# A decoder layer on one core: plain feed-forward tiles over all eight PSUM banks, and another order of VectorE's work before the block products

## The chip, the core and the metric

The kernel runs on one core of one Trainium2 chip. A core has TensorE (PE in the profile), VectorE (DVE), ScalarE (ACT), GpSimd (POOL) and SyncE (SP, which here only issues DMAs). They run side by side, each works through its own list in order, and semaphores tie the lists together. The metric is the device time of one launch in microseconds (us).

## What is computed

One decoder layer on x of 512 tokens by 1024 channels, all in float32: a half-step SwiGLU feed-forward part, a mixing part (pooling and windowed attention, gated and merged), and a second half-step feed-forward part. What the change touches is the feed-forward part, which runs twice:

```python
def swiglu(x, w_gate, w_up, w_down):
    return (jax.nn.silu(x @ w_gate) * (x @ w_up)) @ w_down
...
h = h + 0.5 * swiglu(rmsnorm(h, ffn1_norm), ffn1_w_gate, ffn1_w_up, ffn1_w_down)
...
h = h + 0.5 * swiglu(rmsnorm(h, ffn2_norm), ffn2_w_gate, ffn2_w_up, ffn2_w_down)
```

w_gate and w_up are 1024 x 2816, that is 22 tiles of 128 columns each.

## The kernel before

**Arithmetic.** Every float32 operand is split into a rounded "high" part and a "low" rest (operand minus high), both of type fp32r, and a product is three matmuls: high x high, high x low, low x high (lines 478 to 480 for 512 columns, 531 to 533 for 256). ScalarE makes the highs by copying, GpSimd or VectorE makes the lows by subtracting.

**The plain stage.** The first six tiles f = 0 to 5 of gate and up are multiplied directly. Each is two weight units, u = 2f for gate and 2f + 1 for up: eight slices of 128 x 128, 24 matmuls of 512 columns into one PSUM bank (`plain` and `project` in the tensor block). A unit's way is: SP loads it into one of four slots when the unit four before it has been used (`unit_used`), ScalarE makes its high (`next_unit`, line 850), GpSimd its low (`low_part`, line 1246), PE multiplies. The four banks 4 to 7 are used in turn: tile f writes banks 4 + 2k and 5 + 2k with k = f % 2, so that a unit of tile f waits for `gate_scaled` or `up_scaled` to reach f - 1. Those are counted by VectorE's `plain_scaled` (lines 1378 and 1382), which multiplies a bank by the norm factor rinv and so empties it. ScalarE then makes a tanh (`gate_tanh_tile`, line 878) and VectorE the hidden tile (`plain_hidden`, lines 1389 and 1393). The norm factor comes from a sum over the partitions that PE makes in bank 0 (`sum_of_squares`) and VectorE reads (`norm_factor`).

**The pairs.** The other 16 tiles are multiplied two by two, in eight pairs, by a scheme for 2 x 2 blocks with seven products in place of eight, seven for gate and seven for up. A block product is 12 matmuls of 256 columns, 14 products make a pair (numbered 0 to 13 in the order of `pair`): a11 and a12 of gate, a11 and a12 of up, s2 and s1 of gate, s2 and s1 of up, s3 and s4 of gate, s3 and s4 of up, a22 of gate, a22 of up. Their moving operands are blocks of the normalised input (B11, B21, B22) and four sums of them (NT2, NT1, T3, T4); VectorE builds them (`scale_blocks`, `sum_blocks`), ScalarE makes highs, and VectorE makes seven lows of 128 x 1024 (`block_low`, line 1419, `sum_low`, line 1424), which PE waits for by count (`moving`). Their weights are a1 (a11 and a12), s31 (s1 and s3), s2, s4 and a22. s31 is loaded by SP and then added to in place by an accumulating DMA from GpSimd's queue (`add_units`, line 1252); VectorE adds s2 and s4 from it (`weight_sums`, lines 1431 and 1433) and makes the lows of a1, s2 and s31 (`low_a1`, `low_s2`, `low_s31`, lines 1439, 1443 and 1447); GpSimd makes the "late" lows of s4 and a22 (lines 1257 and 1260). The up blocks of the first pair lie where the units 8 to 11 were, so that SP loads them only as these units are used (`up_prologue`).

**The parts of a pair.** PE adds later products onto banks 0 and 1, and ScalarE copies each intermediate state out (`copy_part`, line 909). PE's s2 of gate waits for the first copy. VectorE adds the copies up (`add_part`, line 1521): g0l and u0l, then g1r (which a22 of gate waits for), g0r, u1r (which a22 of up waits for) and u0r. Between u0l and g1r stand the weight sums and lows for the next pair.

The order on each engine is written out by hand. ScalarE's first part copy of pair 0 stands behind `gate_tanh_tile(5)` and the highs of up's s2 and s31, and waits for `hidden` to reach 6.

## Time and profile before

| | us |
|---|---|
| median of 3 runs | 1081.14 |
| lowest, highest | 1077.69, 1082.23 |
| the profiled execution | 1081.94 |
| its span, first to last instruction | 1080.1 |
| PE busy | 1051.6 |
| VectorE busy | 656.3 |
| ScalarE busy | 478.0 |
| GpSimd busy | 434.1 |
| PE's mean granted clock, of full | 0.992 |

All times in the text are counted from the start of the span. The first feed-forward part (FFN1) has its plain stage up to 89 us and its pairs behind that; the second (FFN2) has its plain stage at 725 to 792. A row of a timeline gives the start, the duration, the engine, the line in the kernel, the operation, what it writes and reads, and how often it follows itself. Rows of one engine overlap a little, since an instruction is let in before the one ahead has ended: the pace is the distance of starts. The idle time before an instruction, and what ended it, stand in brackets. Matmul starts are exact, their ends are modelled.

### The profile page before, as it was taken

Reading aid. Unit: us, or ns where it says so; the run is one execution under the profiler, and the core shown is the slowest. Engines: PE = TensorE matmul, PEld = TensorE weight load, DVE = VectorE, ACT = ScalarE, POOL = GpSimd, SP = SyncE. Lnnn points to the kernel's source line nnn. Section 1 sums busy time; section 2 is a strip of 40 time slices with the busy share of each in tenths; the row PEclk is TensorE's granted clock in tenths of the full one; section 3 lists DMA queues with packets and bytes.
Section 4 is the critical chain, followed back from the end, with each engine's and each line's share of the span. In section 5 each row is a group of like instructions: output and inputs, shape, how many; then the busy total and the mean of one; then the engine's idle time right before and its main releaser. Section 6 shows DMA issues by size and latency. Waiting matters only on the chain.

```text
span 1080.1 us, 15526 instructions
## 1 busy us (share of the span) xinstructions
PE 1051.6 (97%) x6024; PEld 914.7 (85%) x6024; DVE 656.3 (61%) x1008; ACT 478.0 (44%) x825; POOL 434.1 (40%) x240
## 2 busy tenths in 40 slices
PE   6889999999999999999999999999999999999998
PEld 5769999998888777887777788888889999998887
DVE  5899767758440276425676756668986667685101
ACT  6334555556331233335777653343344554553110
POOL 1433342335434435344454535444323423344441
PEclk9999999999999999999999999999999999999999
DMA  7434776733332422222111113216257757433232
GB/s 277 116 97 115 189 196 158 188 106 98 98 98 97 137 88 98 78 78 80 58 58 58 59 59 98 98 39 199 95 119 187 198 163 187 117 104 98 98 98 98
DMA packets 42033, 126.35 MB, mean 117 GB/s; under 512 B 4336, under 2 KB 4336, under 8 KB 41968
## 3 DMA queue, kind: packets, MB, share of 16 engines
q1 hardware_dynamic: 37216, 108.41, 30.3%
q0 software_dynamic: 4608, 16.78, 9.1%
q8 instruction: 45, 0.74, 0.3%
q10 hardware_dynamic: 144, 0.26, 0.1%
q14 instruction: 20, 0.16, 0.1%
HBM read 123.34 MB, written 2.10 MB: 116 GB/s over the span
## 4 chain that ended last, share of the span: by engine, by line
PE 80%; DVE 12%; ACT 3%; DMA 2%; issue 2%; SPq 0%; DVEq 0%; ACTq 0%
PE psum L478 16%; PE psum L480 15%; PE psum L479 15%; PE psum L531 10%; PE psum L532 9%; PE psum L533 9%; PE psum L755 1%; DVE gate L1389 1%; DVE moving_sums_low L1424 1%; PE psum L770 1%; DVE hidden L1393 1%; DMA w_raw<-weights_dram 1%; PE psum L783 1%; DVE u_blocks_low L1419 1%; PE psum L784 1%
## 5 line engine op out<-in xcount | busy, mean ns | idle before, releaser
L1246 POOL TENSOR_TENSOR w_low_in_place<-w_raw,w_high 128x1024 fp32r<-128x1024 f32 x66 | 163.4, 2480 | 209.9 <-ACT w_high L850 209.8
L850 ACT ACTIVATE w_high<-w_raw 128x1024 fp32r<-128x1024 f32 x116 | 122.2, 1055 | 210.6 <-DMA w_raw<-weights_dram 169.0
L1246 POOL TENSOR_TENSOR w_low<-w_raw,w_high 128x1024 fp32r<-128x1024 f32 x50 | 122.7, 2456 | 118.5 <-ACT w_high L850 118.5
L478 PE MATMUL psum<-hidden_high,w_high 128*128 128x512 f32 x352 | 137.0, 389 | 0.0
L479 PE MATMUL psum<-hidden_low,w_high 128*128 128x512 f32 x352 | 137.0, 389 | 0.0
L480 PE MATMUL psum<-hidden_high,w_low_in_place 128*128 128x512 f32 x352 | 136.9, 389 | 0.0
L1356 DVE SCALAR_TENSOR_TENSOR h<-psum,h 128x512 f32<-128x512 f32 x24 | 16.5, 689 | 150.9 <-PE psum L480 150.9
L478 PE MATMUL psum<-u_high,w_high 128*128 128x512 f32 x240 | 99.8, 416 | 0.5 <-DVE u_low L1345 0.5
L479 PE MATMUL psum<-u_low,w_high 128*128 128x512 f32 x240 | 94.4, 394 | 0.0
L480 PE MATMUL psum<-u_high,w_low 128*128 128x512 f32 x240 | 94.4, 394 | 0.0
L478 PE MATMUL psum<-ffn_u_high,w_high 128*128 128x512 f32 x192 | 78.7, 410 | 15.4 <-DVE gate L1378 7.1
L480 PEld LDWEIGHTS psum<-hidden_high,w_low_in_place 128*128 128x128 f32 x352 | 66.1, 188 | 13.8
L479 PEld LDWEIGHTS psum<-hidden_low,w_high 128*128 128x128 f32 x352 | 66.1, 188 | 13.7
L478 PEld LDWEIGHTS psum<-hidden_high,w_high 128*128 128x128 f32 x352 | 66.1, 188 | 13.6
L480 PE MATMUL psum<-ffn_u_high,w_low_in_place 128*128 128x512 f32 x192 | 77.4, 403 | 0.0
L479 PE MATMUL psum<-ffn_u_low,w_high 128*128 128x512 f32 x192 | 77.1, 402 | 0.0
L1485 DVE TENSOR_TENSOR hidden_low<-hidden,hidden_high 128x512 fp32r<-128x512 f32 x44 | 63.7, 1504 | 12.9 <-ACT hidden_high L918 12.9
L1298 POOL TENSOR_TENSOR probs<-probs,inv_denominator 128x1024 f32<-128x1024 f32 x16 | 30.3, 1894 | 71.6 <-DVE inv_denominator L1735 71.6
L478 PEld LDWEIGHTS psum<-ffn_u_high,w_high 128*128 128x128 f32 x192 | 37.7, 196 | 25.3 <-DVE gate L1378 8.0
L478 PEld LDWEIGHTS psum<-u_high,w_high 128*128 128x128 f32 x240 | 45.6, 190 | 13.0 <-DVE u_low L1345 1.7
L531 PE MATMUL psum<-moving_sums_high,gate_s_high 128*128 128x256 f32 x192 | 54.3, 283 | 0.0
L532 PE MATMUL psum<-moving_sums_low,gate_s_high 128*128 128x256 f32 x192 | 54.3, 283 | 0.0
(251 smaller groups left out, 2910.1 us busy)
## 6 DMA issues: line engine op xcount, KB each, us to landing
w_raw<-weights_dram SPq DMA_DIRECT2D x117, 512.0 KB, 3.5
gate_a<-weights_dram SPq DMA_DIRECT2D x16, 512.0 KB, 6.3
gate_s<-weights_dram SPq DMA_DIRECT2D x16, 512.0 KB, 3.6
gate_s<-weights_dram POOLq DMA_DIRECT2D x16, 512.0 KB, 6.4
up_a<-weights_dram SPq DMA_DIRECT2D x16, 512.0 KB, 4.8
up_s<-weights_dram SPq DMA_DIRECT2D x16, 512.0 KB, 3.6
up_s<-weights_dram POOLq DMA_DIRECT2D x16, 512.0 KB, 8.6
gate_a<-weights_dram SPq DMA_DIRECT2D x16, 256.0 KB, 5.3
```

What stands on the lines that cost most here:

```text
L478: pe.matmul(o, wh, xh, start=start, stop=False)
L479: pe.matmul(o, wh, xl, start=False, stop=False)
L480: return pe.matmul(o, wl, xh, start=False, stop=stop)
L531: pe.matmul(o, wh[:, w], xh[:, c, :], start=fresh and c == 0, stop=False, skip_group_check=not fresh)
L532: pe.matmul(o, wh[:, w], xl[:, c, :], start=False, stop=False, skip_group_check=not fresh)
L533: mm = pe.matmul(o, wl[:, w], xh[:, c, :], start=False, stop=c == HALF - 1, skip_group_check=not fresh)
L755: mm = pe.matmul(psum[:, 4 + kv, hh * 2 * BLK:(hh + 1) * 2 * BLK], qs[r, 2 * j + hh, :], ks[r, :], start=(n == 0), stop=(n == 2))
L850: act.activation(high[:, s, :], raw[:, s, :], ACT.Copy).then_inc(high_done, 1)
L1246: pool.tensor_tensor(wlow[:, s, :], raw[:, s, :], high[:, s, :], ALU.subtract).then_inc(low_done, 1)
L1298: pool.tensor_tensor(p, p, rden[:, j % 2, :].unsqueeze(2).to_broadcast([P, 4, 2 * BLK]), ALU.mult).then_inc(probs_ready, 1)
L1356: dve.scalar_tensor_tensor(out=tile(h, c), in0=psum[:, bank, :], scalar=scale, in1=tile(h, c), op0=ALU.mult, op1=ALU.add).then_inc(done, 1)
L1485: dve.tensor_tensor(hid_l[:, f, :], hid[:, f, :], hid_h[:, f, :], ALU.subtract).then_inc(F["hidden_low"], 1)
```

## The change

Three things are changed, in both feed-forward parts.

1. The plain tiles take all eight banks in turn: tile f writes banks `plain_bank(f)` and the next, 4, 6, 0, 2, 4, 6 for f = 0 to 5. Tiles 2 and 3 wait for no scaling any more, tiles 4 and 5 for that of tiles 0 and 1 (f - 3 in place of f - 1). The sum for the norm factor moves to bank 3 in the feed-forward parts, so that in FFN1 the up unit of tile 3 waits until VectorE has read it (`var_ready`). Pair 0 now shares its banks with tiles 2 to 5: a11 waits for the scaling of tile 2, a12 for that of tile 3.
2. VectorE's list from tile 3 on is put in another order (below).
3. ScalarE makes tanh 4 and the high of up's a1 before the highs of gate's s2 and s31, and its first part copy waits for five hidden tiles, the copy of product 5 for the sixth.

```diff
+SUM_BANK = (3, 0, 3)
+def plain_bank(f):
+    return 2 * ((f + 2) % 4)
...
                 for f in range(2, PLAIN[n]):
                     k = f % 2
-                    pe.wait_ge(F["gate_scaled"], f - 1)
-                    project(base + 2 * f, 2 * k, 4 + 2 * k, xh, xl, wlow=raw_low)
-                    pe.wait_ge(F["up_scaled"], f - 1)
-                    project(base + 2 * f + 1, 2 * k + 1, 5 + 2 * k, xh, xl, wlow=raw_low)
+                    if f >= 4:
+                        pe.wait_ge(F["gate_scaled"], f - 3)
+                    project(base + 2 * f, 2 * k, plain_bank(f), xh, xl, wlow=raw_low)
+                    if f >= 4:
+                        pe.wait_ge(F["up_scaled"], f - 3)
+                    elif plain_bank(f) + 1 == SUM_BANK[2 * n]:
+                        pe.wait_ge(var_ready, 2 * n + 1)
+                    project(base + 2 * f + 1, 2 * k + 1, plain_bank(f) + 1, xh, xl, wlow=raw_low)
...
-                        pe.wait_ge(F["up_scaled" if k else "gate_scaled"], PLAIN[n] - 1)
+                        pe.wait_ge(F["up_scaled" if k else "gate_scaled"], PLAIN[n] - 3)
...
+                    else:
+                        pe.wait_ge(F["up_scaled" if k else "gate_scaled"], PLAIN[n] - 2)
...
                 gate_tanh_tile(3, F)
+                gate_tanh_tile(4, F)
+                high_a1(g, up_w)
                 high_s2(g, gate_w)
                 high_s31(g, gate_w)
-                gate_tanh_tile(4, F)
-                high_a1(g, up_w)
                 gate_tanh_tile(5, F)
...
-                    act.wait_ge(F["hidden"], PLAIN[n])
+                    act.wait_ge(F["hidden"], PLAIN[n] - 1)
...
+                else:
+                    act.wait_ge(F["hidden"], PLAIN[n])
                 copy_part(gate_t[:, 1, right], 6)
...
                 plain_hidden(2, F)
                 block_low(n, B11, 1)
                 block_low(n, B21, 2)
-                sum_low(n, NT2, 4)
-                sum_low(n, NT1, 5)
                 plain_scaled(base, 3, F)
                 plain_hidden(3, F)
                 weight_sums(g, gate_w)
                 low_a1(g, gate_w)
+                plain_scaled(base, 4, F)
+                plain_hidden(4, F)
+
+                dve.wait_ge(unit_used, base + 2 * PLAIN[n] - 1)
+                weight_sums(g, up_w)
+                low_a1(g, up_w)
+                sum_low(n, NT2, 4)
+                low_s2(g, gate_w)
+                sum_low(n, NT1, 5)
+                low_s31(g, gate_w)
+                plain_scaled(base, 5, F)
+                low_s2(g, up_w)
+                plain_hidden(5, F)
+                low_s31(g, up_w)
                 sum_low(n, T3, 6)
                 block_low(n, B22, 3)
                 sum_low(n, T4, 7)
-                plain_scaled(base, 4, F)
-                plain_hidden(4, F)
-                low_s2(g, gate_w)
-                low_s31(g, gate_w)
-                plain_scaled(base, 5, F)
-                weight_sums(g, up_w)
-                low_a1(g, up_w)
-                plain_hidden(5, F)
-                low_s2(g, up_w)
-                low_s31(g, up_w)
```

VectorE's list in the middle of the plain stage of FFN1, before; moving_sums_low are NT2, NT1, T3 and T4, u_blocks_low is B22, gate_s and gate_a are the weight blocks of gate:

```order
L1424 TENSOR_TENSOR moving_sums_low<-moving_sums,moving_sums_high 128x1024 [waits moving_blocks_high] x2
L1378 TENSOR_TENSOR gate<-psum,rinv 128x512 [waits unit_used]
L1382 TENSOR_TENSOR up<-psum,rinv 128x512 [waits unit_used]
L1389 SCALAR_TENSOR_TENSOR gate<-tanh,gate 128x512 [waits ffn1_gate_tanh]
L1393 TENSOR_TENSOR hidden<-up,gate 128x512 [waits ffn1_up_scaled,ffn1_gate_silu]
L1431 TENSOR_TENSOR gate_s_80<-gate_s_0_76,gate_a_74 128x512 [waits gate_s31_summed0,gate_a1_landed]
L1433 TENSOR_TENSOR gate_s_0_84<-gate_s_80,gate_a_74 128x512 [waits gate_s2_s4_summed]
L1439 TENSOR_TENSOR gate_a_low<-gate_a_74,gate_a_high 128x1024 [waits gate_s2_s4_summed,gate_blocks_high]
L1424 TENSOR_TENSOR moving_sums_low<-moving_sums,moving_sums_high 128x1024 [waits moving_blocks_high]
L1419 TENSOR_TENSOR u_blocks_low<-u_blocks,u_blocks_high 128x1024 [waits moving_blocks_high]
L1424 TENSOR_TENSOR moving_sums_low<-moving_sums,moving_sums_high 128x1024 [waits moving_blocks_high]
```

The same list in the changed kernel, from gate's low_a1 on (its lines are numbered anew):

```order
L1457 TENSOR_TENSOR gate_a_low<-gate_a_74,gate_a_high 128x1024 [waits gate_s2_s4_summed,gate_blocks_high]
L1396 TENSOR_TENSOR gate<-psum,rinv 128x512 [waits unit_used]
L1400 TENSOR_TENSOR up<-psum,rinv 128x512 [waits unit_used]
L1407 SCALAR_TENSOR_TENSOR gate<-tanh,gate 128x512 [waits ffn1_gate_tanh]
L1411 TENSOR_TENSOR hidden<-up,gate 128x512 [waits ffn1_up_scaled,ffn1_gate_silu]
L1449 TENSOR_TENSOR up_s_99<-up_s_0_95,up_a_93 128x512 [waits up_s31_summed0,up_a1_landed,unit_used]
L1451 TENSOR_TENSOR up_s_0_103<-up_s_99,up_a_93 128x512 [waits up_s2_s4_summed]
L1457 TENSOR_TENSOR up_a_low<-up_a_93,up_a_high 128x1024 [waits up_s2_s4_summed,up_blocks_high]
L1442 TENSOR_TENSOR moving_sums_low<-moving_sums,moving_sums_high 128x1024 [waits moving_blocks_high]
L1461 TENSOR_TENSOR gate_s_low<-gate_s_80,gate_s_high 128x512 [waits gate_blocks_high]
L1442 TENSOR_TENSOR moving_sums_low<-moving_sums,moving_sums_high 128x1024 [waits moving_blocks_high]
L1465 TENSOR_TENSOR gate_s_low_78<-gate_s_0_76,gate_s_high 128x1024 [waits gate_blocks_high]
```

Tile 4 and up's weight sums and low_a1 have moved ahead of the five moving sums and blocks and of gate's low_s2 and low_s31; the two that stood first before, NT2 and NT1, now stand behind the up sums, which wait for the DMAs of up's a1 and s31 and for unit 10.

The end of that list before, up to the first part sum of pair 0 (the last row):

```order
L1378 TENSOR_TENSOR gate<-psum,rinv 128x512 [waits unit_used]
L1382 TENSOR_TENSOR up<-psum,rinv 128x512 [waits unit_used]
L1431 TENSOR_TENSOR up_s_99<-up_s_0_95,up_a_93 128x512 [waits up_s31_summed0,up_a1_landed]
L1433 TENSOR_TENSOR up_s_0_103<-up_s_99,up_a_93 128x512 [waits up_s2_s4_summed]
L1439 TENSOR_TENSOR up_a_low<-up_a_93,up_a_high 128x1024 [waits up_s2_s4_summed,up_blocks_high]
L1389 SCALAR_TENSOR_TENSOR gate<-tanh,gate 128x512 [waits ffn1_gate_tanh]
L1393 TENSOR_TENSOR hidden<-up,gate 128x512 [waits ffn1_up_scaled,ffn1_gate_silu]
L1443 TENSOR_TENSOR up_s_low<-up_s_99,up_s_high 128x512 [waits up_blocks_high]
L1447 TENSOR_TENSOR up_s_low_97<-up_s_0_95,up_s_high 128x1024 [waits up_blocks_high]
L1521 TENSOR_TENSOR gate<-psum,gate 128x256 [waits part_copied,product_done]
```

And in the changed kernel:

```order
L1396 TENSOR_TENSOR gate<-psum,rinv 128x512 [waits unit_used]
L1400 TENSOR_TENSOR up<-psum,rinv 128x512 [waits unit_used]
L1461 TENSOR_TENSOR up_s_low<-up_s_99,up_s_high 128x512 [waits up_blocks_high]
L1407 SCALAR_TENSOR_TENSOR gate<-tanh,gate 128x512 [waits ffn1_gate_tanh]
L1411 TENSOR_TENSOR hidden<-up,gate 128x512 [waits ffn1_up_scaled,ffn1_gate_silu]
L1465 TENSOR_TENSOR up_s_low_97<-up_s_0_95,up_s_high 128x1024 [waits up_blocks_high]
L1442 TENSOR_TENSOR moving_sums_low<-moving_sums,moving_sums_high 128x1024 [waits moving_blocks_high]
L1437 TENSOR_TENSOR u_blocks_low<-u_blocks,u_blocks_high 128x1024 [waits moving_blocks_high]
L1442 TENSOR_TENSOR moving_sums_low<-moving_sums,moving_sums_high 128x1024 [waits moving_blocks_high]
L1541 TENSOR_TENSOR gate<-psum,gate 128x256 [waits part_copied,product_done]
```

Three lows of 128 x 1024 (T3, B22, T4) have come to stand last, directly ahead of the part sums, and the up sums have left this place.

## Rows read from the trace of the kernel before

**Rows 1.** The page, part 1: busy time, share and count of instructions per engine.

```profile
PE 1051.6 (97%) x6024; PEld 914.7 (85%) x6024; DVE 656.3 (61%) x1008; ACT 478.0 (44%) x825; POOL 434.1 (40%) x240
```

**Rows 2.** Timeline of PE, FFN1: start, duration (us), operation, [idle before <- its releaser].

```profile
38.24 0.50 PE L478 MATMUL psum<-ffn_u_high,w_high 128*128 128x512 f32 x1 [3.40 <-DVE gate L1378]
...
76.50 0.50 PE L478 MATMUL psum<-ffn_u_high,w_high 128*128 128x512 f32 x1 [3.71 <-DVE gate L1378]
...
89.11 0.28 PE L531 MATMUL psum<-u_blocks_high,gate_a_high 128*128 128x256 f32 x1
...
92.99 0.39 PE L531 MATMUL psum<-u_blocks_high,up_a_high 128*128 128x256 f32 x1 [0.85 <-DVE up_a_low L1439]
...
107.49 0.28 PE L531 MATMUL psum<-moving_sums_high,gate_a_high 128*128 128x256 f32 x1
...
110.37 0.28 PE L531 MATMUL psum<-u_blocks_high,gate_a_high 128*128 128x256 f32 x1
```

**Rows 3.** Timeline of PE, FFN2: first and third block product, start of pair 1.

```profile
791.55 0.28 PE L531 MATMUL psum<-u_blocks_high,gate_a_high 128*128 128x256 f32 x1
...
796.52 0.39 PE L531 MATMUL psum<-u_blocks_high,up_a_high 128*128 128x256 f32 x1 [1.94 <-DVE up_a_low L1439]
...
815.40 0.28 PE L531 MATMUL psum<-u_blocks_high,gate_a_high 128*128 128x256 f32 x1
```

**Rows 4.** Windows: stretch, length, busy time (x count) per engine, PEclk, DMA share, GB/s.

```profile
45.21:61.53 16.32, 16.32 (x74) 13.51 (x72) 14.25 (x14) 8.52 (x10) 5.20 (x2) 1.00 0.32 97
797.20:800.60 3.40, 3.40 (x18) 3.40 (x17) 2.67 (x4) 2.71 (x6) 1.72 (x1) 0.50 0.96 167
```

**Rows 5.** Timeline of VectorE (DVE), FFN1, plain stage and pair 0.

```profile
73.50 2.35 DVE L1424 TENSOR_TENSOR moving_sums_low<-moving_sums,moving_sums_high 128x1024 fp32r<-128x1024 f32 x2
75.77 0.68 DVE L1378 TENSOR_TENSOR gate<-psum,rinv 128x512 f32<-128x512 f32 x1
...
78.48 0.69 DVE L1431 TENSOR_TENSOR gate_s<-gate_s,gate_a 128x512 f32<-128x512 f32 x1
...
81.14 1.22 DVE L1424 TENSOR_TENSOR moving_sums_low<-moving_sums,moving_sums_high 128x1024 fp32r<-128x1024 f32 x1
82.27 1.22 DVE L1419 TENSOR_TENSOR u_blocks_low<-u_blocks,u_blocks_high 128x1024 fp32r<-128x1024 f32 x1
...
97.61 1.34 DVE L1431 TENSOR_TENSOR gate_s<-gate_s,gate_a 128x512 f32<-128x512 f32 x1 [0.94 <-PE psum L533]
...
102.83 0.68 DVE L1431 TENSOR_TENSOR up_s<-up_s,up_a 128x512 f32<-128x512 f32 x1
...
106.08 0.42 DVE L1521 TENSOR_TENSOR gate<-psum,gate 128x256 f32<-128x256 f32 x1
```

**Rows 6.** Timeline of GpSimd (POOL), FFN1: three lows of units, one late low.

```profile
63.32 8.04 POOL L1246 TENSOR_TENSOR w_low_in_place<-w_raw,w_high 128x1024 fp32r<-128x1024 f32 x3 [7.90 <-ACT w_high L850]
...
97.12 1.28 POOL L1260 TENSOR_TENSOR gate_a_low<-gate_a,gate_a_high 128x512 fp32r<-128x512 f32 x1
```

**Rows 7.** Timeline of ScalarE (ACT), FFN1: high of unit 9, tanh 5, high of up_s31.

```profile
62.20 1.04 ACT L850 ACTIVATE w_high<-w_raw 128x1024 fp32r<-128x1024 f32 x1
...
89.72 0.63 ACT L878 ACTIVATE tanh<-gate 128x512 f32<-128x512 f32 x1 [2.87 <-DVE gate L1378]
...
91.45 1.04 ACT L900 ACTIVATE up_s_high<-up_s 128x1024 fp32r<-128x1024 f32 x1
```

**Rows 8.** Timeline of VectorE, FFN2: the moving lows, the up sums.

```profile
774.83 4.55 DVE L1424 TENSOR_TENSOR moving_sums_low<-moving_sums,moving_sums_high 128x1024 fp32r<-128x1024 f32 x2
...
793.73 0.68 DVE L1431 TENSOR_TENSOR up_s<-up_s,up_a 128x512 f32<-128x512 f32 x1
```

**Rows 9.** Timeline of GpSimd, FFN2: issue of the accumulating DMA.

```profile
785.57 0.87 POOL L1252 DMA_DIRECT2D up_s<-weights_dram  x1 [8.41 <-DMA up_s<-weights_dram]
```

**Rows 10.** DMA issues of 785 to 792: what, queue, count, size, us to landing.

```profile
up_s<-weights_dram POOLq DMA_DIRECT2D x1, 512.0 KB, 6.2
```

**Rows 11.** The tile up_s at 72 to 92, FFN1: us from issue to landing.

```profile
DMA to landing us min/median/max: 3.5/3.6/5.4
```

More of the change, by code:

```diff
@@ L502, in sum_of_squares @@
                 pe.wait_ge(summed[n], DT + 1)
-                pe.matmul(psum[:, 0, :], ones, acc[:, :], start=True, stop=True).then_inc(ss_ready, 1)
+                pe.matmul(psum[:, SUM_BANK[n], :], ones, acc[:, :], start=True, stop=True).then_inc(ss_ready, 1)
             def plain(n, base, F):
@@ L1367, in norm_factor @@
                 dve.wait_ge(ss_ready, n + 1)
-                dve.tensor_scalar(sq[:, 0, :], psum[:, 0, :], 1.0 / D, EPS, ALU.mult, ALU.add).then_inc(var_ready, 1)
+                dve.tensor_scalar(sq[:, 0, :], psum[:, SUM_BANK[n], :], 1.0 / D, EPS, ALU.mult, ALU.add
+                                  ).then_inc(var_ready, 1)
                 dve.wait_ge(root_ready, n + 1)
@@ L1374, in plain_scaled @@
             def plain_scaled(base, f, F):
-                k = f % 2
+                k, bank = f % 2, plain_bank(f)
                 dve.wait_ge(unit_used, base + 2 * f + 1)
-                dve.tensor_tensor(gate_t[:, k, :], psum[:, 4 + 2 * k, :], rinv[:, :], ALU.mult
+                dve.tensor_tensor(gate_t[:, k, :], psum[:, bank, :], rinv[:, :], ALU.mult
                                   ).then_inc(F["gate_scaled"], 1)
                 dve.wait_ge(unit_used, base + 2 * f + 2)
-                dve.tensor_tensor(up[:, k, :], psum[:, 5 + 2 * k, :], rinv[:, :], ALU.mult).then_inc(F["up_scaled"], 1)
+                dve.tensor_tensor(up[:, k, :], psum[:, bank + 1, :], rinv[:, :], ALU.mult).then_inc(F["up_scaled"], 1)
             def plain_hidden(f, F):
```

## The prediction, made before the changed kernel had run

> **What bounds the kernel now.** I read the page's busy shares first: PE is busy 1051.6 of 1080.1 us [rows 1], so a change that leaves PE's work alone can only take the small idle stretches out, or make new ones. PE's timeline shows those of the two stretches that the change touches. FFN1: 3.40 us before unit 4 and 3.71 us before unit 10, both released by VectorE's "gate" (the scaling that empties a bank), and 0.85 us before the third block product, released by up_a_low [rows 2]. FFN2: no wait for a bank at all, only 1.94 us before its third block product [rows 3]. PE pays again behind such a wait: at 797.20 to 800.60 its granted clock is 0.50, the lower level (1.2 GHz), so 3.4 us do the work of 1.7 [rows 4]. Behind the wait of 0.85 us it did not: the ten products from 92.99 to 107.49 took 14.5 us, 1.45 each [rows 2].
>
> Then I read who is behind PE. In FFN1 VectorE runs without a pause from 73.50 to 96.67; the first idle that is listed is 0.94 us before 97.61 [rows 5]. So VectorE is the one that is late, and a free bank lets PE run ahead of it but does not bring its list forward. The place that decides is the far end of that list: product 12 of pair 0 (a22 of gate) needs VectorE's part sum of 106.08, and started at 107.49; pair 1 began at 110.37 [rows 2, 5]. In FFN2 pair 1 began at 815.40 [rows 3]. I follow both to those two points; behind them the pairs run PE-bound, and a shift there is a shift of the end.
>
> **Prices.** A unit is 24 matmuls: 72 in 16.32 us, 5.44 a unit [rows 4]. A block product is 1.44 (two in 107.49 to 110.37) [rows 2]. On VectorE: scale and finish one plain tile 2.71 (75.77 to 78.48), of which the two scalings 1.2; weight_sums with low_a1 2.66 (78.48 to 81.14); one low of 1024 columns 1.14 (81.14 to 82.28); low_s2 0.60 (102.83 to 106.08 holds the up sums, their low and low_s2: 3.25 less 2.66); weight_sums and low_a1 of gate and up and low_s2 for the next pair 5.92 undisturbed (twice 2.66 and 0.60) [rows 5].
>
> **FFN1.** Units 4 to 8 no longer wait for a bank: unit 3 ends at 34.84, so 3.40 us go. But unit 9 needs its low from GpSimd, which is the first of the three at 63.32, so about 66.0 [rows 6], and GpSimd waits there for ScalarE's copies, which end at 62.20 and wait for VectorE's sums, not for PE [rows 7]. Unit 9 to 11 then take 16.3: the first block product starts at 82.3 instead of 89.11, 6.8 us earlier. The 3.71 us before unit 10 and what the clock lost behind both waits are in these 6.8, less what PE now waits for unit 9.
>
> VectorE from 73.50: tile 3 2.71, gate sums and low 2.66, tile 4 2.71: 81.6. The up sums and low 2.66: 84.2, in time for product 2 at 85.2. Then NT2, low_s2, NT1, low_s31 (3 x 1.14 + 0.60): 88.3. Only there stands tile 5's scaling, and ScalarE holds the first part copy behind tile 5's tanh and the two up highs, about 2.0 us (0.63 for the tanh, as much for a copy of that width, 1.04 for the wider one, less their overlap) [rows 7]. It starts its tanh at 88.95 and the part copy is done at about 91.35. PE has finished its first four products at 88.1 and waits 3.3 us for it, a new wait, with half clock behind it (1.7).
>
> VectorE: scaled at 89.5, low_s2 of up at 90.7, tile 5 finished at 92.0, then four lows of 1024 columns (low_s31 of up, T3, B22, T4), which all used to be done before ScalarE's first part copy or early in the stage. Now they meet GpSimd's four late lows of pair 0. What such a meeting costs is in the rows: the three VectorE operations from 97.61 to 102.83 took 5.22 where the same three took 2.66 at 78.48 [rows 5], 0.85 for each; if each of the four waits for one whole GpSimd operation it is 1.28 [rows 6]. So 4.56 plus 3.4 to 5.1: 100.0 to 101.7. The Trainium skill (SBUF — State Buffer, section "Who interferes with whom") says that a DVE instruction with two SBUF inputs and a GpSimd instruction that reads SBUF hold the shared port for the whole instruction; by that rule the upper end holds, and the extra cost of the first of the three in the trace, 1.34 against 0.69 us, is the rest of a GpSimd operation already begun. I take the upper end, since the four GpSimd operations would now be queued back to back: 101.7. Two part sums (0.7) and the 5.92 of the next pair's blocks bring the sum that a22 needs to about 108.7 with its own 0.4 (before 106.5); lower end 107.0. PE by itself would be there at 91.35 + 8 x 1.44 + 1.7 = 104.6, so it waits 2.4 to 4.1 us more, and the clock halves again (1.7). Pair 1 starts at 108.7 + 2.88 + 1.7 = 113.3 at most, 111.6 at least, against 110.37: **+1.2 to +2.9, I take +2.2.** The 6.8 us are all given back.
>
> **FFN2.** PE had no bank wait, so nothing is gained before 791.55. The up sums wait for the accumulating DMA: its issue begins at 785.57 and lands 6.2 us later [rows 9, 10], at 791.8, and it cannot move, since it follows PE's unit 9. Before, VectorE had other work until 793.73 [rows 8]. In the new order it reaches this wait at about 774.83 + 1.3 (a GpSimd low) + 2.71 + 2.66 + 2.4 = 783.9 and stands 7.9 us, with NT2, NT1, T3, B22, T4, gate's low_s2 and low_s31 and tile 5 queued behind it (5 x 1.14 + 0.60 + 1.14 = 7.4 us of work that used to fill this time). The up low is ready at 794.45: product 2 loses its wait of 1.94 and the half clock, 3.6 us gained. But then, as above, 3 x 1.14 + 0.60, tanh, two highs, copy: the copy is done at 801.5, and product 4 started at 801.00 before (796.52 + 2.88 + 1.6 of the half clock). PE waits from 797.3, with the half clock behind it. Tile 5 is finished at 802.2, the four lows at 810.2 to 811.9, the sum for a22 at 817.2 to 818.9 (PE alone: 801.5 + 8 x 1.44 + 1.7 = 814.7), pair 1 at 821.8 to 823.5 against 815.40: +6.4 to +8.1. The same accumulation in FFN1 landed after 5.4 us [rows 11], and FFN2's block before it may come as much sooner: then everything is up to 1.6 earlier. **+4.8 to +8.1, I take +7.0.**
>
> **Sum.** 2.2 + 7.0 = 9.2. FFN1's pair 1 lasted 21.25 us instead of 20.16 because of a late DMA; that might shrink, 0 to -1.1, so I subtract 0.4: +8.8. SP's queue keeps its order; its loads of up blocks in FFN1 come up to 6 us earlier, which nobody needs. The wait for var_ready at unit 7 was met at 27 us and costs nothing. The profiled execution took 1081.94 us (span 1080.1), 0.8 above the median of 1081.14; 1081.14 + 8.8 = 1089.9.
>
> **Rivals.** (a) *The backlog is worked off more cheaply.* If GpSimd's late lows fall beside VectorE's PSUM reads and the DMA lands early, FFN1's sum for a22 is ready at 103.6, PE decides at 104.6 and pair 1 starts at 107.5 (-2.9); FFN2's starts at 817.6 (+2.2) or 816.0. Together -2.3 to -0.7; with half of the meetings about +3. Time 1079 to 1086. For it: the first of the three disturbed operations paid only 0.65. Against: the late lows follow ScalarE's first part copy, which in the walk comes just when VectorE reaches its four lows. Chance 0.24.
> (b) *It does what it is written for.* The lead of 6.8 us in FFN1 is kept and FFN2's 1.94 + 1.7 vanish: -10.4, some 1071. It needs VectorE to deliver the part sum at 99.3, 6.8 us before today, or a22 not to wait for it. VectorE's unbroken row of work from 73.50 speaks against. If only half is kept, 1076. Chance 0.10.
> (c) *The lag runs on.* Pair 1's own chain on VectorE does not absorb it and PE waits again for part sums: another 3 to 6 us in each FFN, about 1096. Chance 0.06.
> (d) The forecast, 1086 to 1094: 0.60.
>
> **How the numbers follow.** A difference under 0.5%, 5.4 us, is what a measurement here can hardly tell from none. Slower by more: (c) and nearly all of (d), 0.64. Within: (a) and the low edge of (d), 0.25. Faster by more: (b), with the last of (a), 0.11. The range leaves out (b) and (c): 1080 to 1094.
>
> **What would show it.** In the new profile: FFN1's first block product near 82 and FFN2's at 791.5; VectorE idle 6 to 8 us before up_s in FFN2, ended by DMA; PE waiting 3 to 4 us before its fifth block product in both FFNs, released by ScalarE's copy; VectorE's four lows of 1024 columns near 2.4 us apart; PE waiting before a22 for a VectorE "gate" sum; four or five stretches of half clock in the two plain stages and their first pairs, where there were three. Wrong if FFN2's pair 1 starts before 817, or if FFN1's starts before 110: then VectorE was not the bound.

## The result and the profile after

| | before | after |
|---|---|---|
| median, us (4 runs each) | 1080.45 | 1089.11 |
| lowest, highest | 1077.69, 1082.23 | 1088.38, 1089.69 |
| ratio, 95% interval | | 1.0082 [1.0061, 1.0104] |
| span of the profiled execution | 1080.1 | 1087.7 |
| the profiled execution | 1081.94 | 1089.69 |

The changed kernel is 0.8% slower: 8.7 us between the medians, where +8.8 was forecast. The sum is right; two of its terms are not, and their errors nearly cancel. Which they are is to be seen in the rows.

The span grew by 7.6 us. PE's own row on the page, part 1 of the profile after (against [rows 1]), says that 2.5 us of this are busy time (the same matmuls, some at the lower clock); the other 5.1 are new idle time:

```profile
PE 1054.1 (97%) x6024; PEld 916.6 (84%) x6024; DVE 662.7 (61%) x1008; ACT 476.8 (44%) x825; POOL 438.9 (40%) x240
```

PE's timeline of FFN1 after the change, every row with an idle time over 0.2 us and the starts that the prediction counts with (against [rows 2]):

```profile
53.19 0.47 PE L486 MATMUL psum<-ffn_u_high,w_high 128*128 128x512 f32 x1 [1.60 <-POOL w_low_in_place L1263]
...
66.28 0.47 PE L486 MATMUL psum<-ffn_u_high,w_high 128*128 128x512 f32 x1 [1.94 <-POOL w_low_in_place L1263]
...
84.37 0.28 PE L544 MATMUL psum<-u_blocks_high,gate_a_high 128*128 128x256 f32 x1
...
92.75 0.36 PE L544 MATMUL psum<-moving_sums_high,gate_s_high 128*128 128x256 f32 x1 [2.47 <-issue]
...
109.43 0.55 PE L544 MATMUL psum<-moving_sums_high,gate_a_high 128*128 128x256 f32 x1 [4.55 <-issue]
...
114.69 0.41 PE L544 MATMUL psum<-u_blocks_high,gate_a_high 128*128 128x256 f32 x1
```

The bank waits are gone. Two waits for GpSimd's lows of units have come, and two in pair 0: before product 4 (s2 of gate) and before product 12 (a22 of gate). Pair 0 now starts 4.7 us earlier than before (89.11) and ends 4.3 us later (110.37). The same timeline in FFN2 (against [rows 3]):

```profile
795.39 0.28 PE L544 MATMUL psum<-u_blocks_high,gate_a_high 128*128 128x256 f32 x1
...
804.04 0.36 PE L544 MATMUL psum<-moving_sums_high,gate_s_high 128*128 128x256 f32 x1 [2.74 <-issue]
...
819.92 0.35 PE L544 MATMUL psum<-moving_sums_high,gate_a_high 128*128 128x256 f32 x1 [2.65 <-issue]
...
823.23 0.28 PE L544 MATMUL psum<-u_blocks_high,gate_a_high 128*128 128x256 f32 x1
```

FFN2 begins later in this kernel, so I count from PE's matmul that sums the squares for the norm, 730.81 us before and 734.65 after. From there the first block product starts at 60.74 us in both kernels, and pair 1 at 84.59 before and 88.58 after: +4.0.

"issue" at product 4 and product 12 does not say that PE had nothing to wait for: the instruction waits for several semaphores, and what ended last has to be looked up on the other engines. ScalarE, whose first part copy ("gate<-psum") ends at 92.64, just ahead of PE's 92.75:

```profile
90.28 0.63 ACT L893 ACTIVATE tanh<-gate 128x512 f32<-128x512 f32 x1 [7.29 <-DVE gate L1396]
90.82 0.61 ACT L911 ACTIVATE up_s_high<-up_s 128x512 fp32r<-128x512 f32 x1
91.34 1.04 ACT L915 ACTIVATE up_s_high<-up_s 128x1024 fp32r<-128x1024 f32 x1
92.28 0.36 ACT L924 ACTIVATE gate<-psum 128x256 f32<-128x256 f32 x1
```

And VectorE in FFN1, from the four lows to g1r, the sum that a22 needs (against [rows 5]); it ends at 109.33, just ahead of 109.43:

```profile
93.40 2.32 DVE L1465 TENSOR_TENSOR up_s_low<-up_s,up_s_high 128x1024 fp32r<-128x1024 f32 x1
95.64 2.31 DVE L1442 TENSOR_TENSOR moving_sums_low<-moving_sums,moving_sums_high 128x1024 fp32r<-128x1024 f32 x1
97.88 2.31 DVE L1437 TENSOR_TENSOR u_blocks_low<-u_blocks,u_blocks_high 128x1024 fp32r<-128x1024 f32 x1
100.11 2.30 DVE L1442 TENSOR_TENSOR moving_sums_low<-moving_sums,moving_sums_high 128x1024 fp32r<-128x1024 f32 x1
102.34 0.41 DVE L1541 TENSOR_TENSOR gate<-psum,gate 128x256 f32<-128x256 f32 x1
...
108.91 0.42 DVE L1541 TENSOR_TENSOR gate<-psum,gate 128x256 f32<-128x256 f32 x1
```

Start to start the four lows are 2.24 us apart, where one alone takes 1.14 [rows 5]. Beside them GpSimd's late lows are as slow: three of the four take 2.27 us, 1.28 in [rows 6]. This one is of after, timeline of GpSimd, FFN1:

```profile
94.61 2.27 POOL L1277 TENSOR_TENSOR gate_a_low<-gate_a,gate_a_high 128x512 fp32r<-128x512 f32 x1
```

In FFN2, VectorE reaches the wait for the accumulating DMA and stands there, with all the lows behind it in its list (against [rows 8], where it had work without a gap):

```profile
794.04 0.69 DVE L1449 TENSOR_TENSOR up_s<-up_s,up_a 128x512 f32<-128x512 f32 x1 [6.50 <-DMA up_s<-weights_dram]
```

Last, PE's granted clock around the waits of FFN1 and FFN2 (windows of after, columns as in [rows 4]):

```profile
67.79:71.20 3.41, 3.41 (x10) 2.63 (x9) 3.41 (x2) 0.00 (x0) 3.41 (x2) 0.50 0.00 0
92.75:95.20 2.45, 2.45 (x20) 2.45 (x21) 2.42 (x3) 2.45 (x6) 1.95 (x2) 1.00 0.98 293
108.75:115.57 6.82, 6.14 (x29) 6.17 (x30) 5.98 (x11) 2.67 (x5) 0.00 (x0) 0.50 0.77 153
805.07:808.48 3.41, 3.41 (x19) 3.41 (x18) 3.41 (x3) 1.49 (x4) 3.41 (x2) 0.50 0.33 135
816.00:823.00 7.00, 4.21 (x34) 3.87 (x33) 6.31 (x11) 1.68 (x3) 1.73 (x2) 1.00 0.86 169
```

The clock is at its lower level (0.50, 1.2 GHz) after the wait at 66.28, for twice 3.41 us from just before the end of the wait at 109.43, and after the wait at 804.04. It is at its upper level behind the waits at 92.75 and 819.92.

So the 7.6 us of span are: FFN1 up to pair 1 +4.3 (of which 0.4 lies ahead of its norm sum, at 25.61 us before and 26.05 after), pair 1 itself -0.7 (20.54 us for 21.25), between pair 2 of FFN1 and the norm sum of FFN2 +0.2, FFN2 up to pair 1 +4.0, and -0.2 at the end.

### The profile page after: what moved, and what is told of

The parts are those of the page before. It is cut to its first block, busy times and chain, and to the rows that moved or that the text cites. A ratio compares the mean times of both kernels' runs of the same rounds, so it can differ in the third digit from the quotient of the medians.

```text
span 1087.7 us, 15526 instructions
## 1 busy us (share of the span) xinstructions
PE 1054.1 (97%) x6024; PEld 916.6 (84%) x6024; DVE 662.7 (61%) x1008; ACT 476.8 (44%) x825; POOL 438.9 (40%) x240
## 4 chain that ended last, share of the span: by engine, by line
PE 84%; DVE 9%; issue 3%; DMA 2%; ACT 1%; POOL 0%; SPq 0%; DVEq 0%; ACTq 0%
PE psum L486 17%; PE psum L488 16%; PE psum L487 16%; PE psum L544 10%; PE psum L546 10%; PE psum L545 10%; DVE window_sums L1661 1%; PE psum L770 1%; PE psum L785 1%; PE psum L798 1%; DMA up_s<-weights_dram 1%; PE psum L800 1%; PE psum L799 1%; DVE u_blocks L1417 1%; DMA w_raw<-weights_dram 1%
## 5 line engine op out<-in xcount | busy, mean ns | idle before, releaser
L546 PE MATMUL psum<-moving_sums_high,gate_s_low 128*128 128x256 f32 x192 | 55.1, 287 | 0.0
```

Of the source, the lines that this page charges most:

```text
L546: mm = pe.matmul(o, wl[:, w], xh[:, c, :], start=False, stop=c == HALF - 1, skip_group_check=not fresh)
```

## The experiments

The theory was: **(T)** the lead that the banks give is worthless, because VectorE's list sets the end of pair 0; the loss comes from the new order of that list, by its idle time in front of the DMA in FFN2, and by four lows that now meet GpSimd's. The rivals: the banks cost or gain something themselves; PE's wait for ScalarE's first part copy is the real cost; the meeting with GpSimd is only a symptom. Each kernel's median is given with its ratio to the kernel before on the same chip (29 runs, 1080.50 us for the first four kernels and 1079.69 for the last four). Where only the two stages are compared, I count "norm sum to pair 1" in each FFN: **84.76 and 84.59 us before, 88.64 and 88.58 after**.

### The banks alone, and the order alone

The first kernel keeps the new banks and puts VectorE's and ScalarE's orders back:

```diff
+                sum_low(n, NT2, 4)
+                sum_low(n, NT1, 5)
...
-                plain_scaled(base, 4, F)
-                plain_hidden(4, F)
-                dve.wait_ge(unit_used, base + 2 * PLAIN[n] - 1)
-                weight_sums(g, up_w)
-                low_a1(g, up_w)
...
+                plain_scaled(base, 5, F)
+                weight_sums(g, up_w)
+                low_a1(g, up_w)
```

> The eight banks and bank 3 for the sum, with VectorE's and ScalarE's orders of the kernel before. Theory A (VectorE's list is the bound, a free bank brings nothing forward): FFN1's first block product starts near 82.5 us, but PE then waits some 7 us before product 2 for up_a_low, whose place in the list has not moved, pair 1 starts at 110 to 113 us, FFN2 does not change; median 1081 to 1084 us. Rival B (the banks are worth the 6.8 us, the new order alone is what costs): FFN1's pair 1 starts near 104 us and the median is near 1074 us.

Measured: 1082.09 us (12 runs), ratio 1.0015 [1.0000, 1.0030]. The lead is there (first block product at 83.78) and is eaten at once by a wait before product 2, PE's timeline of this kernel:

```profile
92.78 0.58 PE L544 MATMUL psum<-u_blocks_high,up_a_high 128*128 128x256 f32 x1 [5.97 <-DVE up_a_low L1455]
```

The low of up's a1 stands behind two plain tiles and five lows in VectorE's old list, and no bank brings it forward. The clock was at its lower level from 90.76 for 6.83 us. Norm sum to pair 1: 86.76 and 85.52 us, 2.0 and 0.9 more than before, where I had expected no change in FFN2 (VectorE's list ran 0.95 us later there from the scaling of tile 3 on; why is not shown). The traced execution is the slowest of the twelve, 4.5 us above their median.

The second kernel is the other half: the old banks, the new orders.

```diff
-                    pe.wait_ge(F["gate_scaled"], f - 3)
+                    pe.wait_ge(F["gate_scaled"], f - 1)
```

> The four banks of the kernel before, with VectorE's and ScalarE's new orders. Theory A: FFN1's first block product only near 87 us, but product 12 at the same place as in the changed kernel, near 109.4 us, since it follows VectorE's list; FFN2 as in the changed kernel; median 1087 to 1090 us, no more than 2 us from the changed kernel. Rival B: the 6.8 us of the banks are missing, median near 1096 us.

Measured: 1088.12 us (6 runs), ratio 1.0066 [1.0041, 1.0091]. With the old banks and their waits (3.40 and 1.38 us) the first block product starts 59.6 us behind the norm sum: 1.3 later than in the full change (58.3), but 3.9 earlier than before (63.5), and earlier than I had expected. The new order alone scales tile 3 sooner, which unit 10 waits for, so it gives PE most of the same lead. Norm sum to pair 1 takes 88.47 and 88.47 us, as in the full change. PE's timeline of this kernel in FFN1 has the same wait before a22 (the code is that of before, so L531):

```profile
107.96 0.55 PE L531 MATMUL psum<-moving_sums_high,gate_a_high 128*128 128x256 f32 x1 [4.55 <-issue]
```

**What follows:** the order makes the whole loss, and the banks make none or very little of it. That was (T)'s reading of the banks: 5 us of lead for PE, nothing at the end.

### Is it the end of VectorE's list?

Three of pair 0's part sums (g1r, g0r, u1r) are moved ahead of the weight sums and lows for pair 1, in both FFNs. Nothing is left out.

```diff
+                if i == 0:
+                    add_part(gate_t[:, 1, right], x, 8, 4)
+                    add_part(gate_t[:, 0, right], 6, 9, 3)
+                    add_part(up[:, 1, right], x + 1, 10, 6)
                 if more:
                     dve.wait_ge(product, done(n, i, 4))
                     weight_sums(g + 1, gate_w)
...
-                add_part(gate_t[:, 1, right], x, 8, 4)
```

> The changed kernel with three part sums of pair 0 (g1r, g0r, u1r) ahead of the weight sums and lows for pair 1 on VectorE, in both FFNs. Theory A (product 12 waits only because VectorE reaches its part sum late): PE's waits of 4.55 and 2.65 us before product 12 vanish with the 6.8 us of half clock behind the first; FFN1's pair 1 starts near 108 us in place of 114.7, FFN2's 2.7 us earlier; median 1079 to 1081 us. Rival C (the time is lost to the wait for ScalarE's copy at product 4 and to the clock, and the wait at product 12 would only move to pair 1's blocks, which now come later on VectorE): median 1087 to 1089 us.

Measured: 1081.68 us (12 runs), ratio 1.0008 [0.9991, 1.0024], against 1.0082 for the full change. VectorE's lows were as slow as before the edit, but its sums for a22 now follow them directly (timeline of VectorE, FFN1):

```profile
99.31 2.31 DVE L1442 TENSOR_TENSOR moving_sums_low<-moving_sums,moving_sums_high 128x1024 fp32r<-128x1024 f32 x1
...
102.21 0.74 DVE L1541 TENSOR_TENSOR gate<-psum,gate 128x256 f32<-128x256 f32 x2
```

g1r is the first of those two adds. a22 started at 105.05 without a wait, norm sum to pair 1 took 81.74 and 85.54 us (6.9 and 3.0 less than after; 0.9 of the 6.9 is not the edit's, since in this execution the clock did not fall behind unit 9, and VectorE's up sums began 55.94 us behind the norm sum and not 56.84). What kept it from the full gain is a new wait, the same in both FFNs, behind product 3 of pair 1 (timeline of PE):

```profile
115.30 0.36 PE L544 MATMUL psum<-moving_sums_high,gate_s_high 128*128 128x256 f32 x1 [1.45 <-ACT gate L924]
```

Pair 1's first copy needs pair 0's hidden tile, and that is now late behind the moved preparation: pair 1 took 21.92 us in both FFNs, for 20.54 and 20.15 after. My expectation had left that out. **What follows:** PE waited before a22 for the part sum and for nothing else; VectorE's list is the bound.

### Is it the idle time before the DMA in FFN2?

In FFN2 alone, six lows are put ahead of the wait for the accumulating DMA:

```diff
+                if n:
+                    sum_low(n, NT2, 4)
+                    low_s2(g, gate_w)
+                    sum_low(n, NT1, 5)
+                    low_s31(g, gate_w)
+                    sum_low(n, T3, 6)
+                    block_low(n, B22, 3)
                 dve.wait_ge(unit_used, base + 2 * PLAIN[n] - 1)
                 weight_sums(g, up_w)
                 low_a1(g, up_w)
```

> The changed kernel, but in FFN2 VectorE does NT2, low_s2 and low_s31 of gate, NT1, T3 and B22 before it waits for the accumulated up block, and not behind it; FFN1 as in the changed kernel. Theory A (FFN2 loses its time because this work is queued behind the DMA): VectorE's idle time before up_s falls from 6.5 us to under 1, no wait before products 2, 4 and 12 of FFN2's pair 0, pair 1 about 7.6 us earlier; median 1081 to 1083 us. Rival C (the DMA wait is hidden by the lead that VectorE has in FFN2): no more than 2 us gained, median 1087 to 1089 us.

Measured: 1079.79 us (12 runs), ratio 0.9994 [0.9979, 1.0009]. The wait for the DMA is nearly filled (timeline of VectorE, FFN2):

```profile
791.77 0.69 DVE L1449 TENSOR_TENSOR up_s<-up_s,up_a 128x512 f32<-128x512 f32 x1 [0.44 <-DMA up_s<-weights_dram]
```

and only 0.67 us are left before a22, none before products 2 and 4. Norm sum to pair 1 in FFN2: 82.14 us, 6.4 less than after and 2.4 less than before, so the new order is worth more than the old one once the list has no hole. FFN1, not edited, stayed at 88.07. It came out 1 to 3 us better than expected, though the stage gained less than the 7.6 us that I had counted on: of the 9.1 us between the spans of the two profiles (1087.7 and 1078.6) 6.4 lie in this stage and 1.8 ahead of FFN1's norm sum (at 24.22 us, 26.05 after), where nothing was edited.

### Both remedies, and one more

The part sums first in FFN1, the lows first in FFN2 (the two diffs above, each in its FFN):

> The changed kernel with the remedy that fits each place: in FFN1 the three part sums ahead of pair 1's weight sums, in FFN2 the work that is ready ahead of the wait for the accumulated up block. Theory A (the two places are independent, each is VectorE's order): the gains of the two separate runs add up but for the 1.45 us wait at pair 1's product 4 in FFN1; median 1073 to 1076 us, faster than the kernel before by 0.4 to 0.7%. Rival C (the stall moves from one place of VectorE's list to the next, so that two remedies are worth no more than one): median 1079 to 1081 us.

Measured: 1077.52 us (12 runs), ratio 0.9984 [0.9971, 0.9996]; norm sum to pair 1 82.77 and 81.99 us. The level is 1.5 us above the expected range, and what was too high is my sum of the two gains: against the profile after, this one gains 5.9 and 6.6 us up to pair 1 and loses 1.4 in pair 1 of FFN1 (the wait of 1.45), 11.1 in all, where the medians differ by 11.6. (The traced execution is the fastest of the twelve.) To remove that wait too, the next kernel finishes pair 0's first hidden tile ahead of up's s2 and s31 lows for pair 1, in FFN1:

```diff
-                if more:
+                late_ups = i == 0 and not n
+                if more and not late_ups:
                     low_s2(g + 1, up_w)
                     low_s31(g + 1, up_w)
...
                 dve.tensor_tensor(hid[:, f, :], gate_t[:, 0, :], up[:, 0, :], ALU.mult).then_inc(pair_hidden, 1)
+                if late_ups:
+                    low_s2(g + 1, up_w)
+                    low_s31(g + 1, up_w)
```

> As the run with both remedies, and in FFN1's pair 0 VectorE makes the hidden tile (the operation that ScalarE's first copy of pair 1 waits for) before low_s2 and low_s31 of up for pair 1. Theory A: PE's wait of 1.45 us before product 4 of pair 1 goes, and the lows that now come 1.4 us later are needed by PE only later; 1 to 1.5 us less than with both remedies, near 1073 us. Rival: the lows come too late for products 6 and 7 and the wait moves there; no difference.

Measured: 1076.31 us (12 runs), ratio 0.9970 [0.9955, 0.9985]. The wait of 1.45 has gone; what is left near that place is this (timeline of PE):

```profile
116.14 0.36 PE L544 MATMUL psum<-moving_sums_high,up_s_high 128*128 128x256 f32 x1 [0.29 <-ACT up L924]
```

But pair 1 of FFN1 took 22.02 us, 21.91 in the kernel ahead: PE now waits 0.67 us before a22 of pair 1 (at 125.68) for VectorE's part sum, so the stall moved down the list, which is what the rival of my expectation says, only at another product. The intervals of the two kernels overlap, so the 1.2 us between their medians are not clear of noise; and what the profile has less in FFN1 lies ahead of the edited place (norm sum to pair 1 81.60 for 82.77), where the clock did not fall behind the wait for product 4. This third move is not shown to be worth anything. The kernel has the lowest median of the study, 0.3% under the one before the change; that lead is clear of its interval, but small, and the level is some 3 us above what I had written.

### What is the meeting with GpSimd worth?

GpSimd's four late lows of pair 0 are left out in both FFNs and ScalarE writes zeros into these tiles instead, so the rests of s4 and a22 are missing from the output. Everything else waits as it did.

```diff
             def late_lows(g, w):
+                if g in (0, PAIRS[0]):
+                    return
                 pool.wait_ge(w["high"], 5 * g + 4)
...
                 act.activation(w["s4_h"][:, :], w["s4"][g % 2][:, :], ACT.Copy).then_inc(w["high"], 1)
+                if g in (0, PAIRS[0]):
+                    act.wait_ge(w["high"], 5 * g + 4)
+                    act.activation(w["s4_l"][g % 2][:, :], w["s4"][g % 2][:, :], ACT.Copy, scale=0.0).then_inc(w["late"], 1)
```

> The changed kernel with GpSimd's four late lows (s4 and a22, gate and up) of pair 0 of both FFNs left out: ScalarE writes zeros in their place, so that this rest of the products is missing from the output. Theory A (these four operations hold VectorE's four lows of 1024 columns up by 1.1 to 1.2 us each): those lows are 1.14 us apart in place of 2.24, the part sum that product 12 waits for comes 4.5 us earlier in FFN1 and 3.4 to 4.5 us in FFN2, pair 1 starts 6 to 8 us earlier in FFN1 (the half clock goes with the wait) and 2.7 us in FFN2; median 1079 to 1082 us. Rival D (VectorE's 2.3 us lows are slow for another reason, such as their operands): no change, 1087 to 1090 us.

Measured: 1078.53 us (11 runs), ratio 0.9989 [0.9979, 0.9999]. VectorE's four lows in FFN1, same places as in the profile after, and g1r behind them:

```profile
93.31 1.22 DVE L1473 TENSOR_TENSOR up_s_low<-up_s,up_s_high 128x1024 fp32r<-128x1024 f32 x1
94.44 1.22 DVE L1450 TENSOR_TENSOR moving_sums_low<-moving_sums,moving_sums_high 128x1024 fp32r<-128x1024 f32 x1
95.58 1.22 DVE L1445 TENSOR_TENSOR u_blocks_low<-u_blocks,u_blocks_high 128x1024 fp32r<-128x1024 f32 x1
96.71 1.22 DVE L1450 TENSOR_TENSOR moving_sums_low<-moving_sums,moving_sums_high 128x1024 fp32r<-128x1024 f32 x1
...
104.42 0.42 DVE L1549 TENSOR_TENSOR gate<-psum,gate 128x256 f32<-128x256 f32 x1
```

They took 4.5 us instead of 8.9, a22 started without a wait, and norm sum to pair 1 fell to 83.02 and 85.28 us (5.6 and 3.3 less; 6 to 8 and 2.7 were expected). **What follows:** the meeting costs VectorE 1.1 us for each of these lows, and in FFN1 it alone makes more than the loss. By the rule that the prediction took from the Trainium skill (SBUF — State Buffer, section "Who interferes with whom"), such a pair of instructions cannot hold the shared port together. The trace agrees: a low pays 1.10 us (2.24 less 1.14), between my two bounds of 0.85 and 1.28 and nearer the upper one.

### Is it the wait for ScalarE's copy?

ScalarE's first part copy is put ahead of tanh 5 and the two up highs:

```diff
                 high_s31(g, gate_w)
+                act.wait_ge(product, done(n, 0, 0))
+                act.wait_ge(F["hidden"], PLAIN[n] - 1)
+                copy_part(gate_t[:, 0, 0:HT], 0)
                 gate_tanh_tile(5, F)
```

> The changed kernel with ScalarE's first part copy of pair 0 ahead of tanh 5 and the two highs of up, so that PE's product 4 need not wait for them. Theory A: the wait of 2.5 us before product 4 (FFN1) and of 2.7 us (FFN2) goes, but product 12 still waits for VectorE's part sum at the same time, in FFN1 for 6 us or more; pair 1 starts within 2 us of the changed kernel in both FFNs; median 1086 to 1090 us. Rival C (the wait for the copy is what costs): each FFN gains its wait and its half clock, median 1080 to 1084 us.

Measured: 1089.81 us (4 runs), ratio 1.0101 [1.0086, 1.0117]. Product 4 no longer waits (88.50 us), but PE then waits four times between products 6 and 9 for 0.3 to 0.7 us, 2.2 in all, a22 of FFN1 waits 4.54 us all the same (I had expected 6 or more), and norm sum to pair 1 is 88.43 us there, 0.2 less than after. In FFN2 it even rose to 90.98, 2.4 more: all four of VectorE's lows now meet GpSimd's (the first takes 2.32 us, 1.22 after), so that g1r and with it a22 come 0.7 us later, and behind the longer wait the clock is at its lower level, where behind the 2.65 us of after it was not, 1.7 more. PE's timeline in FFN2 and the window that begins before it:

```profile
817.83 0.56 PE L544 MATMUL psum<-moving_sums_high,gate_a_high 128*128 128x256 f32 x1 [4.54 <-issue]
```

```profile
815.78:822.61 6.83, 4.78 (x22) 4.81 (x23) 6.02 (x10) 2.67 (x5) 0.86 (x1) 0.50 0.90 159
```

**What follows:** the wait for the copy is real but is no cost of its own. What PE loses there it would lose later.

## Why the prediction was right, and where it was not

**The bound, right.** A lead of PE over VectorE is given back at the last thing that VectorE owes PE (with the banks alone already before product 2, at up's low, and PE waited for nothing behind it). The banks alone changed the time by a ratio of 1.0015 [1.0000, 1.0030], the order alone made 1.0066 [1.0041, 1.0091]. The rival that the change does what it is written for fell with the first of these.

**FFN1's first block product: 82.3 forecast, 84.37 measured.** "Unit 9 at about 66.0" was right (66.28), as was the reason, GpSimd's low. The step that failed is "unit 9 to 11 then take 16.3": the clock fell behind that wait, too, and 3.41 us at 0.50 cost 1.7. I had named PE's wait there and not priced the clock behind it. It reached VectorE, too: SP loads up's s31 when unit 9 is used (issued 47.6 us behind the norm sum here, 46.0 in the kernel with the part sums first), the accumulating DMA follows that, and VectorE, which my walk took through here without a pause, stood 0.86 us for it (timeline of after, FFN1):

```profile
82.89 0.69 DVE L1449 TENSOR_TENSOR up_s<-up_s,up_a 128x512 f32<-128x512 f32 x1 [0.86 <-DMA up_s<-weights_dram]
```

In the kernel with the part sums first the clock stayed up behind unit 9, and VectorE did not wait here.

**Product 4 in FFN1: right in mechanism, 3.3 us forecast, 2.47 measured**, and no half clock followed it.

**The four lows: right in mechanism, near the upper end.** 102.34 measured for the end of the four, 101.7 forecast, but two errors offset each other in it: the lows began at 93.40 and not at 92.0 (0.44 of this lies before the stage, 0.86 is the wait for the DMA) and took 8.94 us and not 9.7, since a meeting cost 1.10 and not 1.28. Behind them VectorE's walk held: the part sum ended at 109.33 against 108.7.

**FFN1's pair 1: +2.2 forecast, range +1.2 to +2.9, +4.3 measured.** The mis-sized term is the clock behind the wait of 4.55 us. I took one stretch of 3.4 us; there were two, 6.83 us, and products 12 and 13 took 5.26 us in place of 2.88: 2.4 instead of 1.7. The rest is the later sum (0.7) and that I had taken 0.7 below my own upper end for no reason that a row gave.

**FFN2's pair 1: +7.0 forecast, range +4.8 to +8.1, +4.0 measured,** outside the range. The steps stood: idle before the DMA (7.9 forecast, 6.50 measured), then the copy, the lows, the sum for a22. (In the walk to that idle time tile 4 stands with 2.4 us, where its price is 2.71; nothing hangs on it, since the DMA decides.) Against the upper end of +8.1, three terms were smaller. The up sums began 1.6 us sooner (59.39 us behind the norm sum; 61.0 by the forecast), half because the DMA landed in 5.4 instead of 6.2 us and half because it was issued 0.9 us sooner, which I had ruled out ("it cannot move"). The row of after's DMA issues, then the issue itself in GpSimd's timeline (785.57 before is 54.8 us behind the norm sum, 788.54 is 53.9):

```profile
up_s<-weights_dram POOLq DMA_DIRECT2D x1, 512.0 KB, 5.4
```

```profile
788.54 0.87 POOL L1269 DMA_DIRECT2D up_s<-weights_dram  x1 [7.64 <-DMA up_s<-weights_dram]
```

The first of the four lows got in ahead of GpSimd's first late low, 1.1 less (in FFN1 GpSimd's was first, and VectorE's took 2.32). VectorE's timeline of after:

```profile
804.55 1.22 DVE L1465 TENSOR_TENSOR up_s_low<-up_s,up_s_high 128x1024 fp32r<-128x1024 f32 x1
805.69 2.31 DVE L1442 TENSOR_TENSOR moving_sums_low<-moving_sums,moving_sums_high 128x1024 fp32r<-128x1024 f32 x1
```

And the clock did not fall behind product 12's wait, so the 1.7 us for it shrank to 0.4. Together 4.0 below +8.1. (The other three lows were 0.5 us cheaper in all, and the next gate sum, which met GpSimd's last late low, 0.4 dearer.) My lower end of +4.8 had the early DMA in it and, at 0.85 a meeting, 7.96 us for the four lows, which took 7.84; what it lacked was that the clock might stay up.

**The sum.** FFN1 2.1 us too low, FFN2 3.0 too high; pair 1 of FFN1 shrank by 0.7 where 0.4 was taken. The terms of the span add up to 7.6, the medians differ by 8.7, and 8.8 was forecast: the fit comes from cancellation, and the error of the walk is 2 to 3 us in each FFN. That the total came within 0.2 us is luck; that the change loses, and at which waits, is not. The two marks set for being wrong, pair 1 before 110 in FFN1 and before 817 in FFN2, were passed at 114.69 and 823.23; the second also counted from the norm sum (86.2 would be the mark, 88.58 it was).

**Rival (a), a cheaper backlog,** had its half in FFN2: the DMA was early and one meeting fell out. **Rival (c), the lag runs on,** did not come: pair 1 in FFN1 took 20.54 us, 14 products at 1.44 and 0.4 of half clock.

## What to carry to other kernels

A buffer that comes free earlier lets its consumer run ahead only as far as the next engine's list lets it: find the engine without idle time and the last entry of its list that the consumer waits for, and time that one. In a list worked off in order, put what is ready ahead of a wait for a DMA, and what the next engine needs now ahead of what it needs next; here two such moves, one of each kind, turned +0.8% into -0.2%. Two-input operations of VectorE moved beside GpSimd operations cost nearly one whole GpSimd operation each here (1.1 us for 1.28), so where a group of them lands matters as much as how early it runs.

## What the runs showed of the hardware that I had not expected

**The clock behind a wait.** A wait of about 2 us sometimes halves it and sometimes not. In the two profiles of this change waits of 1.94 (twice), 2.74, 3.40 and 3.71 us had a stretch of 3.41 us at 0.50 behind them; waits of 1.60, 2.47 and 2.65 did not. Nor did the wait of 1.94 for unit 9 in the kernel with the part sums first, and 2.57 in FFN1 of the kernel with the hidden tile first, where 2.59 at the same place in the kernel ahead of it did. In FFN2 of the order alone a wait of 2.64 did and one of 2.65 did not. A wait of 4.54 or 4.55 us went with 6.83 us at 0.50 in all four places where it came (after, the order alone, and twice in the kernel with the copy first), as did the wait of 5.97 us with the banks alone; in these five places the two products behind the wait took 5.0 to 5.3 us where two take 2.88. What separates 2.57 from 2.59 can't be read from these runs and stays open; I can only say that such a term should carry both values, 0 and 1.7, and a long wait 2.2 to 2.4.

**The two lists take turns.** In FFN1 of the profile after, VectorE's four lows stand 2.24 us apart and three of GpSimd's four late lows take 2.27 us, one starting between each two of VectorE's; the same is seen (2.25 to 2.29 us) in FFN1 of every kernel with the new order and these late lows. Neither engine gets ahead, and a turn takes 0.2 us less than the two lone times together (1.14 and 1.28).
